# Twin-block kernel: the gates' columns of the first projection computed inside the gated recurrence

## The reference, cut to what matters

```
z = rmsnorm(h, mix_norm_g)
p = z @ w_in                                  # 1024 x 7168
y_a = s5_mixer(p[..., :1024], ...)            # a diagonal state-space layer
y_b = hgrn2_mixer(p[..., 1024:2048], p[..., 2048:3072], p[..., 3072:4096], p[..., 4096:5120], ...)
merged = (sigmoid(p[..., 5120:6144]) * (y_a @ w_ssm_proj)
          + sigmoid(p[..., 6144:7168]) * (y_b @ w_hgrn_proj))
h = h + merged @ w_out
```

## Time and profile before

| | |
|---|---|
| median of 3 runs | 3112.19 us (3108.16 to 3113.12) |
| profiled execution, its own time | 3112.08 us |
| its span, first to last instruction | 3110.2 us |
| first stage ends, its last VectorE instruction starts | 370.40 us |
| S5's first load is issued | 373.67 us |
| recurrence's first load is issued | 444.54 us |
| merge's first load is issued | 627.75 us |

### The profile page before, as it was taken

One profiled execution on the slowest core, in us unless ns is written; L12 is line 12 of the kernel. 1 busy time (PEld: TensorE's weight loads), 2 busy tenths in 40 slices (PEclk: granted clock), 3 DMA queues, 4 the chain that ended last, 5 costly groups with the idle time before them and its releaser, 6 DMA issues. The chain is left out here.

```text
span 3110.2 us, 45255 instructions
## 1 busy us (share of the span) xinstructions
PE 2737.7 (88%) x18876; PEld 1972.7 (63%) x18876; DVE 1268.8 (41%) x2146; ACT 801.1 (26%) x1295; POOL 110.6 (4%) x90
## 2 busy tenths in 40 slices
PE   7999877779799969899978999697899889998887
PEld 7999855479799969777867888474333333333332
DVE  5664565534256552366544333663111111111112
ACT  3212135433143331254333333342000000000001
POOL 0000011100000000000001222000000000000000
PEclk9999987789999989999989999898999999999999
DMA  4336530053433344333440000336999999999996
GB/s 136 134 134 155 119 128 21 21 198 124 147 101 115 105 151 123 105 128 130 150 152 29 1 2 1 141 116 257 428 427 428 428 427 428 428 427 428 428 428 254
DMA packets 212406, 628.49 MB, mean 202 GB/s; under 512 B 38464, under 2 KB 125632, under 8 KB 187200
## 3 DMA queue, kind: packets, MB, share of 16 engines
q1 hardware_dynamic: 179712, 573.06, 48.5%
q10 hardware_dynamic: 32512, 52.81, 4.8%
HBM read 577.74 MB, written 45.73 MB: 200 GB/s over the span
## 5 line engine op out<-in xcount | busy, mean ns | idle before, releaser
L3636 PE MATMUL moe_bank<-moe_ring,xg 128*64 128x512 f32 x2048 | 502.8, 636 | 93.8 <-DMA moe_ring<-in_w_exp_up 93.0
L3636 PEld LDWEIGHTS moe_bank<-moe_ring,xg 128*64 128x64 f32 x2048 | 157.4, 144 | 381.2 <-issue 372.7
L3853 DVE TENSOR_TENSOR moe_sg<-moe_sg,moe_bank 64x512 f32<-64x512 f32 x64 | 44.2, 690 | 596.6 <-ACT moe_sg L3747 596.6
L64 PE MATMUL in_bank<-in_x_low,in_w_high 128*128 128x264 f32 x896 | 259.5, 290 | 6.2 <-DVE in_w_low L1194 6.1
L66 PE MATMUL in_bank<-in_x_high,in_w_high 128*128 128x264 f32 x896 | 255.8, 286 | 0.0
L65 PE MATMUL in_bank<-in_x_high,in_w_low 128*128 128x264 f32 x896 | 255.8, 285 | 0.0
L3664 PE MATMUL moe_bank<-moe_ring,moe_act_t 128*64 128x512 f32 x1024 | 230.6, 592 | 0.5 <-ACT moe_act_t L3754 0.5
L64 PE MATMUL up_prod<-up_x_low,up_w_high 128*128 128x264 f32 x704 | 202.0, 287 | 0.0
L66 PE MATMUL up_prod<-up_x_high,up_w_high 128*128 128x264 f32 x704 | 200.9, 285 | 0.0
L65 PE MATMUL up_prod<-up_x_high,up_w_low 128*128 128x264 f32 x704 | 199.5, 283 | 0.0
L64 PEld LDWEIGHTS in_bank<-in_x_low,in_w_high 128*128 128x128 f32 x896 | 169.7, 189 | 8.2 <-DVE in_w_low L1194 7.4
(11 more groups left out here) (522 smaller groups left out, 5375.5 us busy)
## 6 DMA issues: line engine op xcount, KB each, us to landing
moe_ring<-in_w_exp_gate SPq DMA_DIRECT2D x64, 2048.0 KB, 16.7
moe_ring<-in_w_exp_up SPq DMA_DIRECT2D x64, 2048.0 KB, 21.2
moe_ring<-in_w_exp_down SPq DMA_DIRECT2D x64, 2048.0 KB, 23.0
in_w<-in_w_in SPq DMA_DIRECT2D x56, 512.0 KB, 3.5
front_w<-in_w_in SPq DMA_DIRECT2D x50, 512.0 KB, 3.4
up_w<-in_w_up SPq DMA_DIRECT2D x44, 512.0 KB, 5.1
p<-in_out ACTq DMA_DIRECT2D x48, 264.0 KB, 2.0
down_w<-in_w_down SPq DMA_DIRECT2D x8, 1408.0 KB, 8.9
```

The lines of the kernel that those rows point to most:

```text
L64: nc.tensor.matmul(to, w_high, x_low, start=start, stop=False)
L3636: last = nc.tensor.matmul(bank[64 * g:64 * g + 64, s], xe[:, (e // BATCH) % 2, k, at:at + CAPACITY], ring[:, slot_of(n, g), k * HALF:(k + ...
L3853: nc.vector.tensor_tensor(sg[0:CAPACITY, s], sg[0:CAPACITY, s], bank[64:64 + CAPACITY, s], ALU.mult).then_inc(act_ready, 1)
```

## The change

The first stage now computes 40 column tiles (`IN_TILES` = 5 x 1024 / 128). The 16 tiles of the gates (`GATE_TILES`) are computed inside `hgrn2`. There SP loads their weights, ScalarE and VectorE split them (`split_high`, `split_low`), TensorE multiplies them (`gate_products`, the same three passes, in groups of three products), VectorE scales them (`scale_gate`), and SP stores them. 20 of the 256 groups come before the loop over units, 16 of them ahead of the first transposes. The other 236 are spread over 47 steps of the loop, five or six groups a step, between `turn(n + 2)` and `make_scores(n + 1)`.

For this, `x_high`, `x_low` and the scale stay in SBUF until the recurrence ends. The recurrence's PSUM use is packed into six banks, which brings new waits in TensorE's program: `make_scores(n)` for the state before unit n, and `key_values(n)` for the masked scores of unit n and for `finish` of unit n - LATE - 2. `turn_back` moves ahead of `output` and one unit later.

The S5 preparation is packed into 40 slots. Seven slots hold two powers (7, 9, 11, 16, 18, 20, 22), the table's turns overlap the taps, and the 32 small copies go eight to a slot (35 to 38).

```
-IN_TILES = 7 * D_MODEL // P
+IN_TILES = 5 * D_MODEL // P
+GATE_TILES = 2 * D_MODEL // P
...
-                    if S5_SLOT_TOEP <= n < S5_SLOT_TOEP + CHUNK:
+                    if S5_SLOT_TOEP <= n < S5_SLOT_TOEP + CHUNK // 2:
                         sp.wait_ge(taps_ready, 1)
                         sp.wait_ge(toep_zeroed, 1)
+                        for j in range(2 * (n - S5_SLOT_TOEP), 2 * (n - S5_SLOT_TOEP) + 2):
...
-S5_SLOT_ANGLES = 2
-S5_SLOT_INPUT = (7, 30)
-S5_SLOT_TURN = (14, 37)
-S5_SLOT_OUTPUT = (14, 22)
-S5_SLOT_TAPS = (31, 33)
-S5_SLOT_TOEP = 38
-S5_SLOT_TABLE = 46
+S5_SLOT_ANGLES = 1
+S5_SLOT_INPUT = (6, 16)
+S5_SLOT_TURN = (13, 23)
+S5_SLOTS_OUTPUT = (7, 9, 11, 13, 14, 15, 16, 18, 20, 22, 23, 24, 25, 26, 27, 28)
+S5_SLOT_TAPS = (29, 31)
+S5_SLOT_TOEP = 35
+S5_SLOT_TABLE = 29
...
+        def kv_of(j):
+            return (bank[:, 2, 2 * P:3 * P], bank[:, 1, P:2 * P], bank[:, 4, 0:P], bank[:, 5, 0:P])[j]
+        first_groups = groups + 4
+        steps = U + LATE - 4
+        def groups_through(n):
+            rest = GATE_TILES * groups - first_groups
+            return first_groups + min(rest, (n + 1) * rest // steps)
+        def halves_through(n):
+            return groups_through(n) // KT
...
+                def split_high(g):
+                    act.wait_ge(w_loaded[g % 2], 16 * (g // 2 + 1))
+                    if g >= 2:
+                        act.wait_ge(gate_made, 2 * (g - 1))
+                    nc.scalar.copy(w_high[:, g % 2], w[:, g % 2]).then_inc(w_high_ready, 1)
...
                 sigmoid(0)
                 sigmoid(1)
+                split_high(0)
                 log(0)
                 log(1)
+                split_high(1)
...
+                    for half in range(halves_through(n - 1), halves_through(n)):
+                        if half % 2 and half // 2 + 2 < GATE_TILES:
+                            split_high(half // 2 + 2)
...
+                    for half in range(halves_through(n - 1), halves_through(n)):
+                        scale_gate(half // 2, half % 2)
+                        if half % 2 and half // 2 + 2 < GATE_TILES:
+                            split_low(half // 2 + 2)
...
+                    pe.wait_ge(state_ready, states_before(n))
                     nc.tensor.matmul(bank[0:m, 2, 0:2 * m], k_in[:, h % 2, span(i)], qq[:, h % 2, :, span(i)],
...
+                    pe.wait_ge(scores_ready, n + 1)
+                    pe.wait_ge(out_ready, max(0, n - LATE - 1))
...
+                gate_products(0, groups)
                 turn(0)
                 turn(1)
+                gate_products(groups, first_groups)
                 make_scores(0)
                 key_values(0)
-                for n in range(U + LATE):
+                for n in range(U + LATE + 1):
                     if n + 2 < U:
                         turn(n + 2)
+                    gate_products(groups_through(n - 1), groups_through(n))
                     if n + 1 < U:
                         make_scores(n + 1)
+                    if n >= LATE + 1:
+                        turn_back(n - LATE - 1)
                     if n < U:
                         output(n)
                     if n + 1 < U:
                         key_values(n + 1)
-                    if n >= LATE:
-                        turn_back(n - LATE)
```

More of the change, by code:

```diff
@@ L1445, with hgrn2 @@
 HCHUNKS = LEN // HCHUNK
-def hgrn2(nc, stage, p_dram, lb_dram, gain_dram, ident_dram, mask_dram, out_dram):
+def hgrn2(nc, stage, p_dram, lb_dram, gain_dram, ident_dram, mask_dram, out_dram, x_high, x_low, x_scale, w_dram, gates_dram):
     SUPER = 2 * HCHUNK
@@ L1494, in hgrn2 @@
         eps = sb("eps", [P, 1])
+        w = sb("w", [P, 2, KT, P])
+        w_high = sb("w_high", [P, 2, KT, P], F32R)
+        w_low = sb("w_low", [P, 2, KT, P], F32R)
+        gate = sb("gate", [P, 2, LEN])
         bank = ps("bank", [P, 8, 512])
@@ L1532, in hgrn2 @@
         stored = sem("stored")
+        w_loaded = [sem(f"w_loaded{s}") for s in range(2)]
+        w_high_ready = sem("w_high_ready")
+        w_ready = sem("w_ready")
+        gate_made = sem("gate_made")
+        gate_scaled = sem("gate_scaled")
+        gate_stored = [sem(f"gate_stored{s}") for s in range(2)]
+        def kv_of(j):
+            return (bank[:, 2, 2 * P:3 * P], bank[:, 1, P:2 * P], bank[:, 4, 0:P], bank[:, 5, 0:P])[j]
+        half_t = LEN // 2
+        groups = 2 * KT
+        first_groups = groups + 4
[5 more added lines that the diff above has]
+            return groups_through(n) // KT
         def rows(part, h):
@@ L1570, in _ @@
                 sp.wait_ge(stored, 16 * HEADS)
+                for s in range(2):
+                    sp.wait_ge(gate_stored[s], 16 * GATE_TILES // 2)
             @block.scalar
@@ L1643, in _ @@
                 copy_turned(1)
+                split_high(2)
                 for n in range(U + LATE):
@@ L1872, in turn_back, with gate_products @@
                     nc.tensor.transpose(bank[:, 1, 0:m], o_scaled[0:m, n % 2], ident[0:m, 0:m]).then_inc(back_made, 1)
+                def gate_products(first, last):
+                    for at in range(first, last):
+                        g, h, k = at // groups, at // KT % 2, at % KT
+                        if at % groups == 0:
+                            pe.wait_ge(w_ready, g + 1)
+                        if k == 0 and g >= 1:
+                            pe.wait_ge(gate_scaled, 2 * g + h - 1)
+                        tokens = slice(h * half_t, (h + 1) * half_t)
+                        done = three_passes(nc, bank[:, 6 + h, 0:half_t], w_high[:, g % 2, k], w_low[:, g % 2, k],
+                                            x_high[:, k, tokens], x_low[:, k, tokens], k == 0, k == KT - 1)
+                        if k == KT - 1:
+                            done.then_inc(gate_made, 1)
+                gate_products(0, groups)
                 turn(0)
                 turn(1)
+                gate_products(groups, first_groups)
                 make_scores(0)
                 key_values(0)
-                for n in range(U + LATE):
+                for n in range(U + LATE + 1):
                     if n + 2 < U:
                         turn(n + 2)
+                    gate_products(groups_through(n - 1), groups_through(n))
                     if n + 1 < U:
                         make_scores(n + 1)
+                    if n >= LATE + 1:
+                        turn_back(n - LATE - 1)
                     if n < U:
```

89 lines of the change are left out of this document (62 added, 27 removed).

## The result

The changed kernel takes **3133.35 us**, the median of 4 runs (3130.34 to 3136.98), against 3112.22 for the kernel before (3108.16 to 3113.12): a ratio of 1.0071, 95% interval [1.0054, 1.0088]. It is slower by 0.7%. The profiled execution took 3136.98 us, its span is 3135.0 us.

The account below looks back on a forecast made before the run. It took the first stage's end as dense with TensorE products, the recurrence as bound by lower clock and waits among TensorE, ScalarE and VectorE. 3112.1 - 77 (first stage) + 85.5 (recurrence) = 3120.6, stated as 3120.5 us; range 3094 to 3146.

Parts of the forecast that it names:

- waits cost more than the moved tiles: Whole kernel, the forecast's own case: 3120.5 us, with 3109 to 3134 as its range; chance 0.56.
- Sixteen tiles and late slots: First stage: 16 tiles fewer at 5.85 us gain 93.5 us; slots where VectorE is late take back 13.5.
- Toeplitz copies: End of first stage: eight copies a slot delay the next tiles' weights, 3 us, bounds 0 and 8.
- Start: Recurrence before its loop: 48 products at low clock and splits ahead of the first logarithms and sums, +4.5 us.
- Loop: Recurrence's loop: +67 us from TensorE's work and waits (a) to (d), +8 for missing hand-offs.
- (a): Loop: VectorE's split_low waits for ScalarE's split_high, so make_scores comes 1.9 us late, 13 times: 25 us.
- (b): Tenth units: key_values waits for finish behind inverses and a table load, then sums precede the chain; 7 us thrice: 21.
- (c): Loop: sums of the other heads, behind a longer VectorE program, 3 us three times: 9 us.
- (d): Loop: the first head's activations, now with splits behind them: 8 us.
- So already without a wait the loop is 4 us longer: Loop: TensorE's own work, 39 units at 3.86 us on the mean, is 150.5 us.
- the two rivals on the clock: Loop's TensorE clock: it rises to full, 3104.5 us, chance 0.2; or stays near 0.76, 3148.5 us, chance 0.11.
- The gaps take the products: Recurrence: splits and scalings fit other engines' idle time, loop only +4 us, total 3051.5; chance 0.08.

Follow-up runs that it names:

- low_later: The changed kernel with VectorE's split_low one iteration later, behind the next unit's chain and mask: 3107.2 us, ratio 0.9983 to the kernel before.
- first_state_only: low_later with finish directly behind the masked scores, and make_scores waiting only for the first of a unit's four states: 3098.8 us, ratio 0.9958.
- packing_alone: The kernel before with only the recurrence's PSUM packing, its waits and the later turn_back, no gate products there: 3157.3 us, ratio 1.0149.
- all_eased: first_state_only with inverses one iteration later, gate tile 2 split in the loop and its weights loaded ahead of the output gates' loads: 3077.3 us, ratio 0.9883.
- before_inverses_later: The kernel before with only VectorE's reciprocals of ten units' roots taken one iteration later, behind the chain: 3107.2 us, ratio 0.9980.
- toep_small_first: The changed kernel with the 32 Toeplitz copies in five slots from tile 35 (8, 7, 6, 5, 6), not four of eight: 3133.1 us, ratio 1.0060.
- toep_spread: The changed kernel with the 32 Toeplitz copies in six slots from tile 34 (7, 6, 6, 5, 4, 4), not four of eight: 3134.3 us, ratio 1.0071.

## Why the prediction was right, and where it was not

The sign and the case came out, and the size roughly (3120.5 forecast, 3133.35 measured: inside the range to 3146 and just inside the likeliest case's own, to 3134): *waits cost more than the moved tiles*. Going through its steps:

- **Sixteen tiles and late slots** (-93.5, +13.5): right in kind, the slots 2 us too cheap. Tile 34, the last before the copies tell, is finished at 259.71 instead of 244.10, 15.6 us later than before. The double slots are 7.9 us long as worked out, e.g. the `finish` at 88.28 and the next at 96.18:

```profile
88.28 0.71 DVE L1211 TENSOR_TENSOR in_out<-in_bank,x_scale 128x528 f32<-128x528 f32 x1
96.18 0.71 DVE L1211 TENSOR_TENSOR in_out<-in_bank,x_scale 128x528 f32<-128x528 f32 x1
```

- **Toeplitz copies** ("I take 3 us; bounds are 0 and 8"): mis-sized. Tiles 35 to 39 take 38.2 us, 9.0 more than five times 5.85, and equal first stages spread by 2.6 there. But the copies weren't free before: tiles 35 to 55 took 126.3 us, 3.5 more than 21 times 5.85, which my sum leaves out. So the term is 5.5. With the 15.6 above, 93.5 - 15.6 - 5.5 = 72.4. The upper bound adds up to 7.4 from its own terms, not 8; the slack that I took off it wasn't there, since the weights of tile 38 were already late (10.6 us of ScalarE's waiting).
- **S5's first load "at about 296.5"**: 301.20, for these two reasons. **Merge's first load "at about 636"**: 652.11, by this and the next.
- **Start** (+4.5): mis-sized, measured +15.8; this is the largest error of the sum. I counted 48 products at low clock and two splits. Missing was the third pair of splits, which the change puts ahead of the loop, and whose weights SP issues only behind 38 other loads; taking it out of there took 9.2 us off the start (and put 7.3 on the loop).
- **Loop** (+67 + 8): +75.1. That it fits to 0.1 us is luck: the total is righter than its parts.
  - (a) `split_low` behind `split_high`, 25 us: right. 27.5 by low_later; that is 2.3 us for each of the 12 splits in the loop, where 1.9 for each of 13 was worked out.
  - (b) Tenth units, 21 us: half right. The steps there are up to 10.8 us. The wait behind `inverses` and the table load gave 13.2 when taken away (in first_state_only, not in the changed kernel itself), but the other half of my reason, `key_values` waiting for `finish`, gave nothing.
  - (c) and (d), the other heads' sums and the first head: not tested by themselves.
  - "So already without a wait the loop is 4 us longer" (TensorE's 150.5): wrong as the base of the sum. With 63 us of that work out, the loop did not shrink. I took TensorE's stream as the floor on which waits add up; the runs show another, the circle scores, mask, key-values, chain, which alone gives packing_alone a loop of 187.9. I named the new wait of `make_scores` as the place where late chains are felt, and gave it no price of its own. It has one: 12.1 us in the changed kernel for waiting for all four states and not for the first only. All the packing's waits together, without products between, cost 41.4.
- **Drain** (+6): +5.9, right.
- **Signs promised.** Mean steps 5.4: 221.6 / 39 = 5.68. Splits waiting some 2 us: 2.7 (30.1 in 11), and 5.0 to 5.5 at three of them. Clock 0.9 or more: 0.87 in the loop, 0.97 in the drain. It is between the two rivals on the clock, nearer the one in which it rises.
- **The gaps take the products** (3051.5, chance 0.08): wrong for the change as made, yet part of it holds. The products were not what made this loop long. With the waits eased, all_eased is 29.9 us faster (3077.3 to 3107.2) than before_inverses_later. But the gaps don't take them for nothing: there the loop is 33.8 us longer, where the rival has 4, so this kernel is still 26 us above its 3051.5.

## What to carry to other kernels

Work moved into an engine's gaps may cost less than what comes with it: here the operands' preparation on two in-order engines cost 27 us, and the waits that two shared PSUM banks brought 12 to 41. While those waits stood, taking most of the products out gained nothing; with them eased, the moved work still lengthened the loop by 34 us, against 74 gained in the first stage. Before pricing the work, draw the circle of one iteration with every new wait in it, ask which edges are new, and put preparation for a later iteration behind the last thing that the next one waits for. A wait's total in the profile is no promise of a gain: 17.5 us gave nothing, because the next wait took their place; 7.3 gave 13.

## What the runs showed of the hardware

- The granted clock of the same loop was 0.76 before, 0.59 with the packing's waits alone, 0.61 with few gate products, 0.87 with all of them, and 0.97 once waits were eased. As 1.2 GHz reads 0.50 and 2.4 GHz 1.00, these are mixtures of the two levels. It fell where waits were added or products taken out, and the remaining products were slower (133.9 us instead of 116.0 for the same 846 with the packing's waits alone); it rose where waits went. The Trainium skill ("TensorE: Matmul & The Clock Gate", "What's actually happening") calls the low clock the default that activity releases; by that rule, the trace agrees.
- The copies from SBUF to SBUF go in pieces of under 512 bytes, and spreading them over four, five, six or (before) eight slots did not hide them. A load of 512 KB among them took up to 10.7 us from issue to landing (toep_small_first; 8.7 in the changed kernel), against 3.3 to 3.6 in the last tiles of the kernel before. The transfers of the changed kernel from 230 to 300 us:

```profile
DMA packets 10143, 8.75 MB, mean 125 GB/s; under 512 B 7936, under 2 KB 7936, under 8 KB 10072
```

The Trainium skill ("DMA: Bandwidth & Descriptors", "Why small descriptors are slow (HBM only)") exempts such copies from the price of small pieces. By it they would be short, and the kernel before moved only 162 GB/s at a full DMA share among them, which speaks against it. What makes them long stays open: they are in small pieces and each writes only 16 partitions, and no run changes one without the other.

- One program's stretches repeat within about 1 us in the recurrence (start, loop and drain of after, toep_spread and toep_small_first: 280.0, 279.6, 280.6), and only within 3.3 us in the first stage.
